# Expert loops: who issues the loads of the down weights, SyncE or ScalarE

## The reference, cut to what matters

```python
def expert_block(args):
    xb, e = args
    hh = jax.nn.silu(xb @ w_gate[e]) * (xb @ w_up[e])
    return hh @ w_down[e]
ys = lax.map(expert_block, (xs, blk_expert)).reshape(p_slots, d)
y = jnp.zeros((n + 1, d), ys.dtype).at[slot_tok].add(ys * slot_w[:, None])[:n]
```

## Time and profile before

| | |
|---|---|
| median of 3 runs | 2373.58 us |
| profiled execution, whole / its span | 2370.78 us / 2369.0 us |
| PE busy | 2186.3 us (92%) |
| DVE busy / ACT busy | 1080.7 us (46%) / 384.0 us (16%) |
| loads by SP from the expert weights into the ring | 316 of 1 MB, median 18.9 us from issue to landing |
| mean granted clock of TensorE | 0.975 |
| chain that ended last: PE / DMA / SP's queue | 66% / 19% / 9% |

### The profile page before, as it was taken

One profiled execution on the slowest core, in us unless ns is written; L12 is line 12 of the kernel. 1 busy time (PEld: TensorE's weight loads), 2 busy tenths in 40 slices (PEclk: granted clock), 3 DMA queues, 4 the chain that ended last, 5 costly groups with the idle time before them and its releaser, 6 DMA issues.

```text
span 2369.0 us, 27951 instructions
## 1 busy us (share of the span) xinstructions
PE 2186.3 (92%) x10672; PEld 1324.2 (56%) x10672; DVE 1080.7 (46%) x2074; ACT 384.0 (16%) x917; POOL 54.3 (2%) x95
## 2 busy tenths in 40 slices
PE   8999999999999999999999999888999998777776
PEld 7865558854885555884585544343437543333332
DVE  6665647665765665666322433233333343222222
ACT  2211331102210232110301210000003220000001
POOL 1200000000100000000000000000000000000000
PEclk9999999999999999999999999999999999898989
DMA  9542435532953334533592799999997289999998
GB/s 337 190 176 89 160 105 174 202 111 97 301 177 143 125 132 135 171 149 111 167 328 107 295 413 409 417 422 422 422 414 280 107 328 412 416 422 422 422 421 330
DMA packets 223561, 619.39 MB, mean 261 GB/s; under 512 B 16813, under 2 KB 122102, under 8 KB 179558
## 3 DMA queue, kind: packets, MB, share of 16 engines
q1 hardware_dynamic: 216400, 610.26, 67.4%
q0 software_dynamic: 1600, 5.06, 0.6%
q10 hardware_dynamic: 5462, 2.72, 0.4%
HBM read 616.94 MB, written 1.05 MB: 261 GB/s over the span
## 4 chain that ended last, share of the span: by engine, by line
PE 66%; DMA 19%; SPq 9%; DVE 2%; ACT 1%; issue 1%; DVEq 0%; POOL 0%; POOLq 0%; ACTq 0%
PE PS L2787 22%; DMA ring<-expert_parts 19%; PE PS L2870 11%; PE PS L1846 5%; SPq L1133 5%; PE PS L1739 4%; PE PS L2974 3%; PE PS L2928 3%; PE PS L3115 2%; SPq L1130 2%; SPq L1114 1%; PE PS L1799 1%; PE PS L865 1%; PE PS L1310 1%; PE PS L2957 1%
## 5 line engine op out<-in xcount | busy, mean ns | idle before, releaser
L1846 PE MATMUL PS<-ring,arena 128*32 128x512 f32 x1728 | 241.5, 692 | 117.7 <-DMA ring<-expert_parts 115.0
L2787 PE MATMUL PS<-ring,xT 128*128 128x256 f32 x1056 | 243.1, 379 | 3.5 <-ACT xT L2074 3.5
L2787 PEld LDWEIGHTS PS<-ring,xT 128*128 128x128 f32 x1056 | 200.2, 190 | 31.2 <-ACT xT L2074 4.2
L1799 PE MATMUL PS<-arena,xn 128*128 128x128 f32 x1280 | 203.2, 297 | 13.0 <-DVE h L1645 13.0
L1846 PEld LDWEIGHTS PS<-ring,arena 128*32 128x32 f32 x1728 | 64.1, 124 | 266.7 <-issue 239.1
L1799 PEld LDWEIGHTS PS<-arena,xn 128*128 128x128 f32 x1280 | 164.0, 189 | 73.1 <-issue 41.3
L2787 PE MATMUL PS<-arena,xn 128*128 128x256 f32 x704 | 165.7, 379 | 0.0
L1652 DVE TENSOR_TENSOR arena<-PS,small 128x512 f32<-128x512 f32 x62 | 42.8, 691 | 269.0 <-PE PS L1799 269.0
L2870 PE MATMUL PS<-ring,arena 128*128 128x512 f32 x352 | 162.8, 592 | 0.0
L2787 PEld LDWEIGHTS PS<-arena,xn 128*128 128x128 f32 x704 | 130.6, 190 | 16.1
L1815 PE MATMUL PS<-arena 128*128 128x512 f32 (+1 forms) x300 | 138.4, 603 | 0.0
(11 more groups left out here) (433 smaller groups left out, 2886.5 us busy)
## 6 DMA issues: line engine op xcount, KB each, us to landing
ring<-expert_parts SPq DMA_DIRECT2D x316, 1024.0 KB, 18.9
ring<-ffn_gate_up SPq DMA_DIRECT2D x88, 1024.0 KB, 10.4
ring<-ffn_down SPq DMA_DIRECT2D x44, 1024.0 KB, 7.3
arena<-expert_parts SPq DMA_DIRECT2D x73, 256.0 KB, 12.3
arena<-expert_parts SPq DMA_DIRECT2D x13, 1024.0 KB, 13.4
ring<-w_in SPq DMA_DIRECT2D x16, 768.0 KB, 6.0
ring<-conv_w_in SPq DMA_DIRECT2D x12, 1024.0 KB, 12.7
ring<-expert_parts SPq DMA_DIRECT2D x16, 512.0 KB, 15.2
```

What stands on the lines that cost most here:

```text
L1799: last = mm(PS[:, bank, at * P:(at + 1) * P], lhsT=xn[0:w, t, k * P:(k + 1) * P], rhs=onehot[0:w, t, :], start=t == 0, stop=t == nt - 1)
L1846: last = mm(PS[BLK * j:BLK * (j + 1), 2, :], lhsT=xgT[:, k, j * BLK:(j + 1) * BLK], rhs=w[k % HALF], start=k == 0, stop=k == KD - 1)
L2787: last = mm(out, lhsT=a[:, k, :], rhs=b[:, 256 * k:256 * (k + 1)], start=k == 0, stop=k == 3)
```

## The change

In both mixtures, SP's loop no longer waits for `dn_used` and no longer issues the down parts. ScalarE's loop does it: before it does group g it waits for the down products of group g-1, reads the four expert numbers and issues the four down parts of group g into its own DMA queue. The group at `WRITTEN` and the last group are taken out of ScalarE's loop, because their down parts are still issued by SP. The addresses, sizes and semaphores that the loads raise are the same.

```diff
@@ fetched (SP) @@
                     for j in range(GROUP):
                         gate_up(bass.ds(es[j], 1), j, half)
+                if not in_halves:
+                    return
                 sp.wait_ge(M[i].dn_used, g * 2 * GROUP)
-                if not in_halves:
-                    for j in range(GROUP):
-                        down(bass.ds(es[j], 1), j)
-                    return
@@ moe_act (ACT) @@
-            with act.Fori(WRITTEN[i], groups) as g:
+            final = act.value_load(ng_last[0:1, 0:1], min_val=NE // GROUP - 1, max_val=MAX_GROUPS - 1)
+            group(WRITTEN[i])
+            with act.Fori(WRITTEN[i] + 1, final) as g:
+                act.wait_ge(M[i].dn_used, g * 2 * GROUP)
+                for j in range(GROUP):
+                    e = act.value_load(eid[0:1, bass.ds(g * GROUP + j, 1)], min_val=0, max_val=NE - 1)
+                    src = A["expert_parts"][i][bass.ds(e, 1)]
+                    act.dma_start(ring[:, j, 2 * PART:3 * PART], src[:, 2].rearrange("o p w -> p (o w)")).then_inc(M[i].dn_loaded, 16)
                 group(g)
+            group(final)
```

## The result

The changed kernel takes 2379.58 us (median of 9 runs, 2376.59 to 2381.33). The kernel before, run beside it on the same chip, takes 2372.02 us (9 runs). The ratio is 1.0033, 95% interval 1.0023 to 1.0044, so the change costs 7.6 us, or 5.5 to 10.4. The profiled execution took 2379.4 us with a span of 2377.6: 8.6 us more than the one before. Predicted were 2379.6 us; how much of that closeness is luck, the part on the prediction says.

What follows compares the result with a forecast made beforehand. Transfers were taken to bound both expert loops (DMA share 1.01, 421 GB/s). Terms 0 + 0 + 5 + 1 = +6 us on 2370.78 give 2376.8, and 2.8 more for the median 2379.6 us; 8-in-10 range 2372 to 2389.

Steps and rivals of the forecast that it cites:

- SyncE loses waits and loads: In both expert loops SyncE drops 16 waits and 64 loads, covered by PE's 7.46 us of gather products: value 0.
- ScalarE's work: Per group, four reads and four issues, 4.4 us, fit into ScalarE's 16.77 us idle before the up products: value 0.
- When ScalarE's batch begins to move: In the loops, ScalarE's down batch begins to move 4.5 us after the down products, with 3 us of start-up.
- The turns of the queues: In the first layer's loop, queues share by halves, so up 8 lands at t = 38.0 instead of 29.9; PE waits 8 us more.
- PE runs 4 to 7 us late in the loop: In the first layer's loop, up products start 6.7, 4.3, then 5.2 us late, while DMA is never idle.
- The end of the first layer: At the first layer's last group, lateness of 4.3 to 6.7 us leaves 3.5 to 6 after 0.78 of wait: +5 us.
- The second layer: At the second layer's end, 5.2 to 6.9 us of waits and slow clock absorb lateness; 0 to 2 remain: +1 us.
- The sum: Over the whole kernel: 0 + 0 + 5 + 1 = +6 us on the profiled 2370.78 us; 2379.6 us for the median.
- Nothing changes: Rival, both loops: ACT's loads come late or behind SP's and slack absorbs the lateness; 0 to +2 us, 2374.5; chance 0.20.
- The queues run dry: Rival, both loops: both queues empty for a moment in each group, 11 us on top of the 6, 2391; chance 0.17.
- Faster: Rival, both loops: two queues fill small gaps at the changes between loads; -7 us, 2366.5; chance 0.08.
- The signs: In the loops: down loads about 13 us, up loads 25 or more, fewer longer PE waits, share 1.0, last up products 5 us late.

Runs made afterwards that it cites:

- e8_group14_only: Against the kernel before: ScalarE issues the down loads of group 14 of the first layer alone; 2379.62 us against 2370.67, ratio 1.0039.
- e3_act_reads_only: Against the changed kernel: ScalarE keeps the wait, four reads and cut loop, but SyncE issues all loads; 2371.47 us, ratio 1.0001 to the kernel before.
- The experiments with one and two parts: As the changed kernel, but ScalarE issues only one or two of each group's four down loads, SyncE the others; 2373.36 and 2376.38 us against 2370.67.
- e2_layer1_only: As the changed kernel, but the down loads move to ScalarE in the second layer only; 2372.20 us, ratio 0.9997 to the kernel before.
- e7_after_gather: As the changed kernel, but ScalarE also waits for the gather products before issuing the down loads; 2398.18 us against 2370.67, ratio 1.0113.
- e4_last_two_on_sp: As the changed kernel, but SyncE issues the down loads of the first layer's groups 13 and 14; 2371.24 us, ratio 0.9998 to the kernel before.

## Why the prediction was right, step by step

- **SyncE loses waits and loads, value 0.** No run speaks against it (`e8_group14_only` takes the wait and four loads from SyncE and only loses time); none tests it alone.
- **ScalarE's work, value 0.** Right (`e3_act_reads_only`).
- **When ScalarE's batch begins to move.** Right: 4.5 us after the down products was the working. They end at 1531.26 + 3.64 = 1534.90 in the changed kernel; up to 1539.3 only SyncE's queue (q1) moves packets, and from 1539.5 to 1540.5 both do.
- **The turns of the queues.** Right. In the changed kernel's first group of the loop the last up load takes 31.27 us instead of 21.45, and PE starts at 1557.27. The working gave t = 38.0 after 1518.25, so 1556.3: 1.0 us off, of which 0.5 was there before the loop (the up products of group 7 start at 1518.74). The experiments with one and two parts and `e8_group14_only` show that it is this delay that costs. The halves were a choice; the packets of the two queues confirm them (last section). The Trainium skill (DMA: Bandwidth & Descriptors, Queues, rings and completion order) says that an engine takes turns between queues by packets, and the counts agree: 463 packets and 465 in 16 us.
- **PE runs 4 to 7 us late in the loop.** Nearly: the starts of the up products are 9.1, 7.1, 5.2, 8.3 and 8.3 us after the kernel before at groups 8, 10, 11, 12 and 14. Of each, 0.5 was there before the loop. And the working had the DMA engines never idle, with 4.3 us of lateness at group 10; the lull of 1574 to 1591 lies just ahead of that group and adds up to the estimated 1.9 us. With both taken off, about 6 of the 8.3 us at group 14 are the passing itself, inside the forecast.
- **The end of the first layer, +5 us.** The mechanism was right and the size too small: 1767.23 against 1756.99 is 10.2 us. The term was lateness (4.3 to 6.7) minus 0.8. The lateness was 8.3, for the two reasons just given, and the last period didn't shrink to 29.05 us but took 31.73 (1735.50 to 1767.23). Its up products ran 6.39 us instead of 3.64, at the lower clock after the long wait. I had named this price for the loop and left it out of the last group.
- **The second layer, +1 us.** It was 0 (`e2_layer1_only`, -2.8 to +1.4): the lateness is taken. The sentence that the last halves are issued 25 us ahead of the landing holds for the first of them (2330.40, with the last landing at about 2355.9); the last was issued by 2345.96, 10 us ahead.
- **The sum.** +6 was forecast, +8.6 came in the profiled execution and +7.6 in the medians. That 2379.6 was named and 2379.58 measured is luck: the loss was 1.6 us larger than forecast, and the 9 runs of the kernel before gave 2372.02 where the forecast started from 2373.58. Of the first layer's 10.2, 0.5 was there before the loop began, and 1.5 came back in the mixer behind it. That part isn't the change's doing, as the last section shows.
- **The rivals.** *Nothing changes* fell with the interval. The Trainium skill's rule (DMA: Bandwidth & Descriptors, Rules for kernel authors) that spreading loads over engines gives no bandwidth holds, with a share of 1.01 before and after. But that rule is about bandwidth, and here the order was the loss. *The queues run dry* happened once, for about 2 us in the loop's second group, and not in each group as the rival had it; `e7_after_gather` shows it in full at 0.95. *Faster* didn't happen.
- **The signs.** ScalarE's loads at 13 us, fewer and longer waits of PE (11.4 us in the first loop, 14.4 in the second), and the share at 1.0 came as named. That the up loads would rise to 25 us or more came only in every second group (31.3, 24.9, 27.4 and 26.6 at groups 8, 10, 12 and 14; 14.1, 20.4 and 17.4 at 9, 11 and 13), and the last up products were to be 5 us late and were 10.2.

## What to carry to other kernels

Where transfers are the bound at a share of 1 and each batch lands just ahead of its use, one queue is a schedule: it delivers in the order of issue. A second queue keeps the bytes and breaks the order, so before moving loads to another engine, ask which load of the first queue they will pass and who waits for that one. And a wait that grew inside such a loop costs little until the last group, as long as the transfers go on; look there for the room, then read what it costs (0.8 us of room in one layer, over 5 by the prediction's working in the other). Check too that the lateness doesn't keep the next loads from being issued: here it did once.

## What the runs showed of the hardware

- **Turns between the queues come out even.** While the up loads (q1, SyncE's) and the down loads (q10, ScalarE's) of the loop's first group are both under way, from 1541 to 1557 in the changed kernel, the queues moved (packets, MB, share of 16 engines):

```profile
q10 hardware_dynamic: 463, 3.40, 51.1%
q1 hardware_dynamic: 465, 3.38, 50.6%
```

All these loads are of 1 MB and the same form. ScalarE's four landed 14.7 us after their issue in the median. The sum of both stayed what one queue moved. The stretch 1539 to 1558 of the changed kernel (columns as in the earlier trace rows):

```profile
1539.00:1558.00 19.00, 7.58 (x56) 3.61 (x58) 4.51 (x15) 0.00 (x0) 0.00 (x0) 0.79 1.01 422
```

- **A clock dip of 1.5 us comes and goes.** In the mixer behind the first layer PE waits 1.93 us for VectorE in both kernels. In the kernel before, the granted clock then falls to the lower level for a while (0.81 in the mean of 9 us); in the changed one it doesn't. Of before, and of after:

```profile
1834.00:1843.00 9.00, 7.07 (x32) 5.67 (x30) 4.05 (x12) 2.22 (x9) 0.00 (x0) 0.81 0.00 0
```

```profile
1844.00:1853.00 9.00, 7.07 (x40) 5.72 (x38) 5.62 (x16) 2.70 (x9) 0.00 (x0) 1.00 0.00 0
```

PE does 40 matmuls in the second and 32 in the first. `e3_act_reads_only`, which has no lateness, also gains 1.5 us at this place, and `e4_last_two_on_sp` doesn't. So a single profile scatters by this much, and a difference of 1.5 us between two profiles is no evidence. What decides whether the dip comes stays open.
